# Moving part of a causal convolution from VectorE to GpSimd in the recurrent mixer

## What is computed

```python
glu = c_val * jax.nn.sigmoid(c_gate)                     # 256 tokens x 512 channels
conv = lax.conv_general_dilated(                         # causal, one 31-tap filter per channel
    glu, conv_w[:, None, :], window_strides=(1,), padding=[(CONV_WIDTH - 1, 0)],
    dimension_numbers=('NWC', 'WIO', 'NWC'), feature_group_count=D_CONV) + conv_b
y_b = jax.nn.silu(layer_norm(conv, conv_ln_g, conv_ln_b, CONV_LN_EPS))
return jnp.concatenate([y_a, y_b], axis=-1) @ w_out      # y_a: the recurrence
```

## Time and profile before

| | before |
|---|---|
| median of 3 runs | 2383.51 us |
| lowest and highest run | 2381.48 and 2385.42 us |
| the profiled execution: its time | 2382.13 us |
| the profiled execution: its span | 2380.3 us |
| PE busy, whole span | 2335.3 us (98%) |
| DVE busy, whole span | 1788.5 us (75%) |
| ACT busy, whole span | 1197.8 us (50%) |
| POOL busy, whole span | 120.6 us (5%) |

### The profile page before, as it was taken

How to read it: one execution, slowest core, us unless ns; L and a number is a source line. 1 busy time by engine, 2 the same in 40 slices (tenths; PEclk the granted TensorE clock), 3 DMA queues, 4 the chain that set the end, 5 groups by cost and what they waited for, 6 DMA issues and landing times.

```text
span 2380.3 us, 27847 instructions
## 1 busy us (share of the span) xinstructions
PE 2335.3 (98%) x11426; PEld 1932.5 (81%) x11426; DVE 1788.5 (75%) x1849; ACT 1197.8 (50%) x1413; POOL 120.6 (5%) x145
## 2 busy tenths in 40 slices
PE   9999999999999999999999999999999999999998
PEld 8888877888878888788887887798888888777887
DVE  7875867787787756677787876797877777656875
ACT  5553455365455443644554554534455455555453
POOL 0001000000000010000001002102000000110000
PEclk9999999999999999999999999999999999999999
DMA  9566534565555655365564666304466466343563
GB/s 307 176 229 205 181 106 169 185 218 190 194 188 191 231 197 179 124 225 172 198 225 147 202 210 221 93 1 142 159 213 230 159 212 213 124 159 129 173 200 117
DMA packets 281439, 428.10 MB, mean 180 GB/s; under 512 B 11795, under 2 KB 193683, under 8 KB 281184
## 3 DMA queue, kind: packets, MB, share of 16 engines
q1 hardware_dynamic: 273136, 399.51, 49.6%
q0 software_dynamic: 7632, 26.29, 3.5%
q10 hardware_dynamic: 544, 0.52, 0.1%
HBM read 423.41 MB, written 1.05 MB: 178 GB/s over the span
## 4 chain that ended last, share of the span: by engine, by line
PE 76%; DVE 13%; ACT 5%; DMA 3%; issue 2%; POOL 1%; SPq 0%; POOLq 0%; DVEq 0%; ACTq 0%
PE bank L2093 18%; PE bank L2095 18%; PE bank L2094 18%; DVE wl L1199 6%; PE bank L2185 4%; PE bank L2189 4%; PE bank L2188 4%; ACT wh L629 2%; PE bank L2619 2%; DMA wf<-in_ffn_w_up 1%; PE bank L2140 1%; DMA wf<-in_ffn_w 1%; POOL rstd L469 1%; DVE arena L1799 1%; PE bank L2162 1%
## 5 line engine op out<-in xcount | busy, mean ns | idle before, releaser
L2093 PE MATMUL bank<-wh,xTh 128*128 128x512 f32 x1824 | 723.2, 396 | 9.8 <-DVE xTl L1252 4.0
L1199 DVE TENSOR_TENSOR wl<-wf,wh 128x2048 fp32r<-128x2048 f32 x267 | 605.8, 2286 | 162.6 <-ACT wh L629 162.2
L2095 PE MATMUL bank<-wh,xTl 128*128 128x512 f32 x1824 | 710.0, 389 | 0.0
L2094 PE MATMUL bank<-wl,xTh 128*128 128x512 f32 x1824 | 709.0, 389 | 0.0
L629 ACT ACTIVATE wh<-wf 128x2048 fp32r<-128x2048 f32 x267 | 506.7, 1915 | 175.7 <-PE bank L2095 67.3
L2093 PEld LDWEIGHTS bank<-wh,xTh 128*128 128x128 f32 x1824 | 342.9, 188 | 81.4 <-DVE xTl L1252 5.3
L2095 PEld LDWEIGHTS bank<-wh,xTl 128*128 128x128 f32 x1824 | 342.6, 188 | 72.6
L2094 PEld LDWEIGHTS bank<-wl,xTh 128*128 128x128 f32 x1824 | 343.3, 188 | 67.4 <-issue 0.7
L2093 PE MATMUL bank<-wh,hTh 128*128 128x512 f32 x704 | 277.3, 394 | 0.2
L2095 PE MATMUL bank<-wh,hTl 128*128 128x512 f32 x704 | 275.1, 391 | 0.0
L2094 PE MATMUL bank<-wl,hTh 128*128 128x512 f32 x704 | 274.8, 390 | 0.0
(11 more groups left out here) (368 smaller groups left out, 2589.9 us busy)
## 6 DMA issues: line engine op xcount, KB each, us to landing
wf<-in_ffn_w SPq DMA_DIRECT2D x136, 512.0 KB, 6.0
wf<-in_w_in SPq DMA_DIRECT2D x52, 1024.0 KB, 5.6
wf<-in_ffn_w_gate SPq DMA_DIRECT2D x68, 512.0 KB, 5.9
wf<-in_ffn_w_up SPq DMA_DIRECT2D x68, 512.0 KB, 6.9
wf<-in_ffn_w SPq DMA_DIRECT2D x28, 1024.0 KB, 7.1
wf<-in_ffn_w_down SPq DMA_DIRECT2D x28, 1024.0 KB, 7.7
arena<-in_ffn_w SPq DMA_DIRECT2D x38, 512.0 KB, 7.8
arena<-in_ffn_w SPq DMA_DIRECT2D x16, 1024.0 KB, 5.9
```

The lines of the kernel that those rows point to most:

```text
L1199: dve.tensor_tensor(wl[s], wf[s], wh[s].bitcast(f32), ALU.subtract).then_inc(SEM[f"lo{s}"], 1)
L2093: pe.matmul(o, lh, rh, start=start, stop=False)
L2094: pe.matmul(o, lh, rl, start=False, stop=False)
L2095: return pe.matmul(o, ll, rh, start=False, stop=stop)
```

## The change

The two upper groups of channels (`ct` 2 and 3) are made by POOL for the taps 0 to 21. POOL has one instruction over both groups (128x512) for a product with the weight, and one for the sum: for tap 0 the product goes into `conv_o` and the bias is added, and for each later tap the product goes to the new tile `tap_o` and is added to `conv_o`. That is 44 instructions, behind the two bonus products. DVE keeps all 31 taps for the groups 0 and 1, and makes the taps 22 to 30 of the groups 2 and 3 at the merges 18 to 21 (`LATE_TAPS`), behind a wait for POOL's `conv_done`. `taps_at` has other counts, each tap now being two instructions. PE waits for both engines. The distance in the wait of a tap on DVE's own semaphore goes from 3 to 1, since two groups alternate in place of four.

```diff
+        def weight(j):
+            return convw[:, 2:4, j:j + 1].broadcast_to([P, 2, T])
+
+        pool.wait_ge(SEM["gluT_ready"], c.next("gluT_ready", TB))
+        pool.wait_ge(SEM["cw_ready"], c.next("cw_ready"))
+        pool.wait_ge(SEM["gram_ready"], c.next("gram_ready", 4))
+        product(conv_o[:, 2:4, :], gluT[:, 2:4, 0:T], weight(0))
+        product(conv_o[:, 2:4, :], conv_o[:, 2:4, :], weight(CONV), ALU.add)
+        for j in range(1, POOL_TAPS):
+            product(tap_o, gluT[:, 2:4, j:j + T], weight(j))
+            product(conv_o[:, 2:4, :], conv_o[:, 2:4, :], tap_o, ALU.add)
+        pool.sem_inc(SEM["conv_done"], 1)
         pool.wait_ge(SEM["bonus_done"], c.next("bonus_done"))
...
-        def tap(j):
-            for ct in range(4):
-                dve.wait_ge(SEM["dve"], c.so_far("dve") - 3)
+        def tap(j, groups):
+            for ct in groups:
+                dve.wait_ge(SEM["dve"], c.so_far("dve") - 1)
...
         def taps_at(i):
-            if i < 2 or i > 21:
-                return 0
-            return 2 if i > 3 and (i % 2 or i in (18, 20)) else 1
+            return 0 if i < 2 or i > 20 else 1 if i in (2, 4, 6, 8, 10, 12, 14) else 2
 
         j = 0
+        LATE_TAPS = {18: range(22, 24), 19: range(24, 26), 20: range(26, 28), 21: range(28, CONV), 22: (), 23: ()}
...
             for _ in range(taps_at(i)):
-                tap(j)
+                tap(j, range(2))
                 j += 1
+            if i == 18:
+                dve.wait_ge(SEM["conv_done"], c.next("conv_done"))
+            if i > 17:
+                for k in LATE_TAPS[i]:
+                    tap(k, range(2, 4))
...
-        pe.wait_ge(SEM["conv_done"], c.next("conv_done"))
+        pe.wait_ge(SEM["conv_done"], c.next("conv_done", 2))
```

More of the change, by code:

```diff
@@ L228, in program @@
     conv_o = part(7168, 4, T)
+    tap_o = part(6656, 2, T)
+    POOL_TAPS = 22
     rho = part(8192, TB, RW)
```

## The result

The kernel became slower, by about the forecast amount. The median is 2395.72 us (2391.90 to 2398.11, 5 runs) against 2383.51 of the kernel before, +12.2 us. The ratio on record is 1.0054 (95% interval 1.0043 to 1.0065); the two medians alone give 1.0051. Against the 25 runs of the kernel before that stand beside the experiments (median 2382.73 in one series, 2382.76 in the other) it is +13.0.

A forecast was written before the change was run, and what follows sets the result against it. PE was taken to bound the kernel, with 0.97 us idle in the merges. Losses of 8.8, less 0.3 slack and 0.3 gain, plus 1.7 for the clock, made +10 on 2383.5: 2393.5 us, range 2385.5 to 2404.

The forecast's parts named there:

- PE bound with 0.97 us to give: In the merges, 1541 to 1630, PE is busy 88.03 of 89.00 us, so 0.97 us is the most to gain.
- POOL's own work, 52.3 us: POOL's 23 products at 1.115 and 21 sums at 1.27 us take 52.3 us, done alone at 1598.0.
- A tap waits for one POOL instruction: In DVE's bursts, a first tap takes 0.75 us, each other 1.21; a pair of merges takes 8.74 us.
- the short pair of merges 10 and 11: PE's pair of 5.91 us at merges 10 and 11 loses 2.8 us, where ordinary pairs lose 1.4.
- The pair 2 and 3 has slack: At merges 2 and 3 DVE has few taps and waits for PE; about 0.3 us is taken off the loss.
- One clock fall that is felt, +1.7: In the merges PE's clock falls once behind its idle time, costing 1.7 us (ends 0 and 8.5).
- +0.3 for the gain: In the merges PE loses part of its waits for DVE, a gain of 0.3 us (ends 0 and 0.97).
- (a): DVE's taps go in consecutively while POOL waits; POOL is late at merge 18, 9.9 us of stall: 2395 us, chance 0.20.
- (b): At DVE's taps the loser waits whole, then pays full length; a pair takes 10.6 us: 2402.5 us, chance 0.10.
- (c): Beside DVE's taps a POOL instruction counts only 0.9 to 1.0 us: about +3, 2386.5 us, chance 0.10.
- (d): Taps beside POOL still take 0.475 us; only 0.3 (at most 0.97) us is gained: 2383 us, chance 0.08.
- (e): The kernel gets faster by more than 0.2%, 4.8 us, needing the mixer's end to come much earlier; chance 0.02.

The follow-up runs named there:

- the second experiment: The changed kernel with DVE's taps 1 to 24 of groups 0 and 1 left out (merges 3 to 17), POOL's 44 instructions kept: 2381.68 us, ratio 0.9998.

## Why the prediction was right

The forecast was 2393.5 us with a range of 2385.5 to 2404, from a mechanism that held. By its steps:

- **PE bound with 0.97 us to give.** Right. With POOL idle and the taps gone from DVE the kernel gains 1.4 us by the medians, with none inside the interval. So a loss was all that could be had, and its size was the question.
- **POOL's own work, 52.3 us.** Low by 1.8. At its prices alone it takes 23 x 1.12 + 21 x 1.35 = 54.1 (the second experiment: 54.9, with 0.9 spent behind the addition). The product's price was right (1.12 with its wait). The sum of two full operands, priced at 1.27 with its wait as half of a 128x1024 one, takes 1.35: 1.27 and its 0.08. The error had no effect on the end of it worth naming: POOL ended at 1601.7, not 1599, still ahead of merge 18.
- **A tap waits for one POOL instruction.** Right, and the term that carried the forecast. The burst of two took 2.15 (forecast 0.75 + 1.21 = 1.96), the burst of four 4.58 (0.75 + 3 x 1.21 = 4.38), a mean pair 9.04 against 8.74. The small gap is the longer sum: half of 2.59, POOL's cycle, is 1.30 and not 1.21. For the five pairs 4 to 13 the loss is 8.8 us. That the forecast also had 8.8 is in part luck. It counted 5.3 pairs at 1.4, and 1.4 more for the short pair of merges 10 and 11. Measured are five pairs that lose 1.75 in the mean, and the short one 1.73 (8.89 against 7.16): its extra did not come, since on DVE that pair was as long as the others before.
- **The pair 2 and 3 has slack.** Wrong, and this is the step that failed. It was counted as a gain of 0.3 and cost 4.1. Three things were passed over. The largest, 3.5 us, is the burst: it has four tap instructions like those of the later odd merges, its first one behind a POOL instruction of 2.14, and "six per pair" is not true here, where DVE loses only two first taps. The two TENSOR_SCALAR first taps that are left read one SBUF tensor and were held up all the same, by 0.9 net of the two that are gone; the earlier trace rows had shown a TENSOR_SCALAR, of 8 elements, that took 1.64 until POOL's product ended. The addition to `rv_t` is a two-operand instruction too, and cost 0.3. The slack was not there either: before, DVE waited only 0.51 us for PE ahead of merge 4's mask.
- **One clock fall that is felt, +1.7.** Wrong in the other direction. The clock fell, for 6.8 and 3.4 us in the profiled execution, but at most 0.3 us of it reached the end, as DVE was the late engine. The prediction had this in the upper end of its range ("hidden in good part since DVE is late anyway") and not in its value.
- **+0.3 for the gain.** Not seen: the waits behind merge 14 are as they were.

The sum of the forecast was 8.8 - 0.3 - 0.3 + 1.7 = 9.9, or 10; that of the measurement is 8.8 + 4.1 + 0 = 12.9 in the stretch and 12.2 in the medians. The errors, +4.4 for the first pair, -1.7 for the clock and +0.3 for the gain, partly cancelled, which is luck. What is left is 3.0 in the stretch; the median lies 2.2 above 2393.5.

The rivals fell as follows. (a), DVE keeps its place through a burst: POOL's timeline shows one POOL instruction between any two taps, and DVE does not idle at merge 18. The run with instructions half as long shows (a)'s stall by another way. (b), nothing overlaps: its pair of 10.6 was measured at 9.04. (c), POOL frees its reading side early: a tap costs POOL's whole cycle, not less. (By its own prices (c) comes to 4 x 0.7 + 2.1 - 0.6 = 4.3 and not to 3.) (d), no interference: refuted by the mean of 793 ns. (e) would have needed time that PE did not have. Where the Trainium skill, SBUF — State Buffer, section "Who interferes with whom", has the second to issue blocked until the first has finished, the rows agree in that a tap waits for a whole instruction of POOL's. They differ from the word-for-word reading of (b) in what the loser pays then: POOL's product and sum beside taps are recorded at 1.10 and 1.33, 0.06 above their 1.04 and 1.27 alone, and not with a tap of 0.4 added. That the loser's start overlaps was in the earlier trace rows, and the difference between (b) and the forecast rested on it.

## What to carry to other kernels

Before moving element-wise work to GpSimd, look at what VectorE does at the same time: if its instructions read SBUF twice (or are of the tensor-with-scalar form, as the two first taps here) and GpSimd's read SBUF, each of VectorE's waits for a whole one of GpSimd's, and moving half of the work can lengthen the list it was taken from. Count that list from the first instruction at which both are active, the pair where the overlap begins included, and count a slower clock only on the engine that ends last. If the work must go there, short GpSimd instructions released into VectorE's PSUM-reading stretches cost nothing here (2382.9 us), where the same ones running freely cost 3 us; but first ask what the bounding engine has to give, which was 0.97 us.

## What the runs showed of the hardware that was not expected

- The two engines alternate one for one, although a tap waits only for the one before the last, which is done by then: a burst of four took 4.66 us with three whole instructions of POOL's between them and the rest of one ahead.
- The toll is very unequal. POOL's cycle for a tap is 2.59 us with two of DVE's taps let in and 2.47 alone, so a tap costs POOL about 0.06; the same meeting costs DVE 1.3 in place of 0.4.
- A DVE instruction with one tensor operand in SBUF (TENSOR_SCALAR with a per-partition scalar, 128x256) is held up as well: two took 2.27 us, where four took 1.37. Why that form is held up was not tested.
- POOL's sum of two full operands of 128x512 takes 1.27, its product with a broadcast weight 1.04; at 128x256 the two take 0.72 and 0.61. Halving an instruction costs about a fifth more in all.
- 88 memsets of 0.525 us on POOL cost DVE's taps nothing (476 ns).
- The granted clock fell to 1.2 GHz behind idle times of PE of 2.79 and 2.23 us in the kernel after, and not behind one of 1.34. The length of the wait does not decide it alone: ahead of the merges PE idled for 1.87 us in both traces, and the clock fell in the one before and not in the one after. In the run where PE waited 12.4 us, the clock fell 4.1 us into the wait and was low for 13.7 us, 8.3 of them in the wait and 5.4 behind it.
